# Latent attention of a hybrid encoder: prompt tiles taken from the last (512 keys) to the first (128 keys)

## What is computed

```python
q_n = m_qn.reshape(b, t, MLA_HEADS, MLA_NOPE_DIM)          # 64 wide
q_p = rope(m_qr.reshape(b, t, MLA_HEADS, MLA_ROPE_DIM), pos)  # 32 wide
k_n = jnp.einsum('bsc,chd->bshd', c_all, mla_w_uk)
v_c = jnp.einsum('bsc,chd->bshd', c_all, mla_w_uv)
s = (jnp.einsum('bqhd,bkhd->bhqk', q_n, k_n)
     + jnp.einsum('bqhr,bkr->bhqk', q_p, k_pe)).astype(jnp.float32) * MLA_SCALE
s = jnp.where(mask, s, -jnp.inf)      # prompt: key_chunk <= q_chunk, chunks of 64
probs = jax.nn.softmax(s, axis=-1).astype(v.dtype)
o = jnp.einsum('bhqk,bkhd->bqhd', probs, v)
```

## Time and profile before

| what | value |
|---|---|
| runs | 1555.78, 1557.09, 1557.13 us; median 1557.09 us |
| profiled execution, its own time | 1557.62 us |
| its span (first to last instruction) | 1555.8 us |
| PE, DVE, POOL, ACT busy | 97%, 66%, 53%, 44% of the span |
| MLA stage in layer 0 | iteration 18 begins at 236.24 us, the last output part at 308.00 us |
| PE's idle time in that stage | 0.99, 0.76, 0.84 and 0.59 us |
| granted clock of PE | 1.00 in that stage, 0.997 over the span |

### The profile page before, as it was taken

One profiled execution on the slowest core, in us unless ns is written; L12 is line 12 of the kernel. 1 busy time (PEld: TensorE's weight loads), 2 busy tenths in 40 slices (PEclk: granted clock), 3 DMA queues, 4 the chain that ended last, 5 costly groups with the idle time before them and its releaser, 6 DMA issues.

```text
span 1555.8 us, 33898 instructions
## 1 busy us (share of the span) xinstructions
PE 1512.2 (97%) x14202; PEld 1432.6 (92%) x14202; DVE 1027.9 (66%) x1750; ACT 681.4 (44%) x1204; POOL 832.3 (53%) x468
## 2 busy tenths in 40 slices
PE   7999999999999999999999999999999999999997
PEld 6989888799999999999998898878999999999996
DVE  6866556646848668586677655675488594766955
ACT  6621434344534344455455223344454443434553
POOL 3344111175765949578643441113659477594973
PEclk9999999999999999999999999999999999999998
DMA  6211011243241422322322110114323324142122
GB/s 204 70 54 41 17 58 42 51 118 96 77 140 42 137 68 86 105 68 98 103 80 69 43 43 15 58 46 70 113 92 95 96 75 140 46 136 68 46 91 85
DMA packets 45128, 123.81 MB, mean 80 GB/s; under 512 B 10992, under 2 KB 15856, under 8 KB 44720
## 3 DMA queue, kind: packets, MB, share of 16 engines
q1 hardware_dynamic: 44688, 119.86, 25.7%
q10 hardware_dynamic: 288, 1.78, 0.3%
HBM read 117.86 MB, written 3.76 MB: 78 GB/s over the span
## 4 chain that ended last, share of the span: by engine, by line
PE 77%; DVE 13%; POOL 5%; ACT 3%; issue 2%; DMA 0%; SPq 0%; DVEq 0%; ACTq 0%; POOLq 0%
PE psum_p L1811 38%; PE psum_t L1868 17%; PE psum_p L1884 6%; PE psum_t L1920 6%; POOL w_rest L810 3%; DVE conv_out L1339 2%; PE psum_p L1847 2%; PE psum_p L2068 1%; PE psum_p L2048 1%; POOL w_rest L798 1%; PE psum_t L2032 1%; PE psum_t L2039 1%; PE psum_t L1904 1%; DVE mla_q L1369 1%; PE psum_p L1904 1%
## 5 line engine op out<-in xcount | busy, mean ns | idle before, releaser
L1811 PE MATMUL psum_p<-hidden,w_high 128*128 128x272 f32 x3680 | 618.3, 290 | 5.4 <-POOL w_rest L798 4.1
L1811 PEld LDWEIGHTS psum_p<-hidden,w_high 128*128 128x128 f32 x3680 | 519.5, 188 | 10.3 <-POOL w_rest L798 6.0
L798 POOL TENSOR_TENSOR w_rest<-raw,w_high 128x1024 fp32r<-128x1024 f32 x110 | 268.9, 2448 | 397.6 <-ACT w_high L927 397.6
L1811 PE MATMUL psum_p<-hidden,w_rest 128*128 128x272 f32 x1840 | 379.8, 288 | 0.0
L1811 PEld LDWEIGHTS psum_p<-hidden,w_rest 128*128 128x128 f32 x1840 | 288.4, 188 | 0.0
L810 POOL TENSOR_TENSOR w_rest<-w_sums,w_high 128x512 fp32r<-128x512 f32 x128 | 208.0, 1650 | 93.3 <-DVE w_sums L1594 55.3
L927 ACT ACTIVATE w_high<-raw 128x1024 fp32r<-128x1024 f32 x112 | 117.9, 1055 | 153.7 <-PE psum_p L1811 103.4
L1868 PE MATMUL psum_t<-hidden_split_a,w_high 128*128 128x272 f32 x896 | 178.6, 290 | 2.1 <-issue 1.0
L1868 PE MATMUL psum_t<-hidden_split_b,w_high 128*128 128x272 f32 x896 | 177.0, 288 | 0.4 <-DVE hidden_split_b L1610 0.4
L1868 PEld LDWEIGHTS psum_t<-hidden_split_a,w_high 128*128 128x128 f32 x896 | 140.0, 188 | 5.8 <-issue 4.5
L1868 PEld LDWEIGHTS psum_t<-hidden_split_b,w_high 128*128 128x128 f32 x896 | 140.3, 188 | 0.8 <-DVE hidden_split_b L1610 0.8
(11 more groups left out here) (307 smaller groups left out, 2627.2 us busy)
## 6 DMA issues: line engine op xcount, KB each, us to landing
raw<-w_units SPq DMA_DIRECT2D x146, 512.0 KB, 3.6
raw_more<-w_units SPq DMA_DIRECT2D x64, 512.0 KB, 3.5
x<-x_t SPq DMA_DIRECT2D x8, 272.0 KB, 6.7
y_t<-y SPq DMA_DIRECT2D x8, 272.0 KB, 2.2
constants<-consts ACTq DMA_DIRECT2D x1, 1088.0 KB, 9.3
ple_in<-p_t SPq DMA_DIRECT2D x2, 544.0 KB, 11.7
constants<-consts SPq DMA_DIRECT2D x1, 1088.0 KB, 6.1
constants<-consts ACTq DMA_DIRECT2D x1, 649.5 KB, 6.2
```

Source lines behind the costliest of these rows:

```text
L798: mark(pool.tensor_tensor(wlo_at(l, s, 2), raw_at(l, u), whi_at(l, s, 2).bitcast(F32), ALU.subtract), lo_done)
L1811: ins = pe.matmul(pp[:, 2 * b + h, 0:HALF], w(l, s, 2)[:, cols(k)], rhs[:, k, part, h * HALF:(h + 1) * HALF], start=(n == 0 and z == 0), s ...
```

## The change

The prompt's MLA tasks come in the order of tiles 3, 2, 1, 0, and the sample's four stay last. Tasks 18 to 21 then have 512 keys, 22 to 25 have 384, 26 to 29 have 256 and 30 to 33 have 128. All else in the schedule stays at its iteration. The second hunk keeps the PSUM bank's wait on the tile that was split before. No instruction is added or removed.

```diff
+MLA_ORDER = (3, 2, 1, 0, 4)
+
+
 def tasks():
     out = [("swa", n, g) for n in range(NCH) for g in range(2)]
-    out += [("mla", i, h) for i in range(SEQ // P + 1) for h in range(4)]
+    out += [("mla", i, h) for i in MLA_ORDER for h in range(4)]
     return out
...
                 rows, first_key, keys = task_shape(kind, i)
-                last_group = [mixed.at(l, i if kind == "swa" else NCH + i)] if h1 == 1 and t > 1 else []
+                last_group = [mixed.at(l, i if kind == "swa" else NCH + MLA_ORDER.index(i))] if h1 == 1 and t > 1 else []
                 wait_apart(pe, pcopy.at(l, t + 1), *last_group)
```

## The result

The changed kernel takes 1564.29 us (median of five runs, 1562.66 to 1564.42), against 1557.13 us before (five runs, 1555.78 to 1557.68). The ratio is 1.0046, with a 95% interval of 1.0036 to 1.0057: 7.2 us slower. The forecast was 1562.8, in a range from 1556.8 to 1566.8.

A forecast was written before the change was run, and what follows sets the result against it. PE, 97% busy, was taken as the bound, except in B, set by DVE. A +5.6, B -1.8, C -1.0 make +2.8 us a layer, +5.7 in two, giving 1562.8 us; range 1556.8 to 1566.8.

The forecast's parts named there:

- B: Latent attention, 271.58 to 294.71 us, until output feature tile 1 starts: set by DVE, 23.13 falls to 21.34 us.
- The long wait: PE's wait for DVE before the output part's tile 1, forecast as most of 4.4 us of waits in B.
- POOL's hold: In B, DVE scalings started inside POOL's rest end only after it: 1.50 us against 0.49.
- Both scalings that were to be held: DVE's scalings of tasks 28 and 32 in B, forecast to end after POOL's rests; the 128-key one 1.3 to 1.5 us.
- A: Latent attention, 233.42 to 271.58 us, to the last quarter of iteration 28's unit: PE-bound, longer by 5.6 us a layer.
- the scores' price: PE's scores per task: 512 keys 0.56 us above 128, 384 keys 0.11 above 256; +2.35 us in A.
- C: Latent attention, 294.71 to 308.00 us, until the last tiles start: PE's own, shorter by 1.0 us a layer.
- the turn of task 33 and the values: PE's work in C: turn of task 33 and values of 32 and 33, -0.33 - 0.65 = -1.0 us.
- No change: Rival, chance 0.18: PE, busiest over the whole span, keeps all its work; time 1557 to 1559 us.
- Faster: Rival, chance 0.12: DVE reaches `mixed_a` before PE, both PE waits in B vanish, -1.60 us a layer; 1553.9 us.
- Much slower: Rival, chance 0.05: 512-key tasks meet chain steps; PE waits about 1 us in each of iterations 18 to 25; 1573 us.

The follow-up runs named there:

- dve_B: Changed kernel plus two unused DVE operations of 128x544 in iteration 31 of each layer, inside B; 1568.78 us.
- late_after: Changed kernel, but ACT rounds the second output unit's weights in iteration 35, not 32, so POOL's rest moves out of B; 1562.90 us.
- last0: Kernel before, with the prompt's tiles in the order 1, 2, 3, 0; 1561.62 us, ratio 1.0036.
- last3: Kernel before, with the prompt's tiles in the order 2, 1, 0, 3; 1561.45 us, ratio 1.0034.
- the filled kernel: Changed kernel plus five unused fp32 PE matmuls of 128x256 a layer, where PE waits in B; 1562.77 us, ratio 1.0040 to the kernel before.

## Why the prediction was right, and which terms were off

The order costs 2.84 us a layer by the forecast and 3.47 by the rows at full clock. The difference, 1.3 us in two layers, is most of what lies between the forecast 1562.8 and the measured 1564.29.

**B, the main step, held.** PE's work in it was forecast at 16.9 us and measured 16.93; its waits at 4.4 and 4.26; B at 21.34 and 21.20. The long wait ended with L1312, and the waits for ACT lay before scores and a turn. But the long wait was 1.70 us of the 4.26, not most of it. The waits for ACT came to 2.01, and a wait of 0.55, at the values of the next tile, was not foreseen: they write the PSUM bank that DVE was still splitting. That DVE sets B is shown by dve_B, that POOL's hold lies in its chain by late_after. Both scalings that were to be held were held. The second took 1.70 us and not 1.3 to 1.5. Of a rest of 2.38 us 1.49 would have been left at 0.89 us after its start, and the scaling of rows 12 ended 0.29 behind its rest, so the rows themselves gave 1.8. The rest took 2.51, of which 1.62 lay after the scaling's start, and 0.08 came behind it.

**A was mis-sized, +6.0 for +5.6.** The failed term is the scores' price. The earlier trace rows gave 604 and 326 ns, but these stood in two places: 512 keys in B, 128 keys in A. After the change each size stands in the other's place:

```profile
L2042 PE MATMUL psum_t<-mla_k,mla_q 96*128 96x512 f32 x8 | 4.5, 644 | 0.0
L2042 PE MATMUL psum_t<-mla_k,mla_q 96*128 96x384 f32 x8 | 3.6, 538 | 0.0
...
L2042 PE MATMUL psum_t<-mla_k,mla_q 96*128 96x256 f32 x8 | 2.4, 379 | 0.0
L2042 PE MATMUL psum_t<-mla_k,mla_q 96*128 96x128 f32 x8 | 1.6, 286 | 1.1 <-ACT probs L1061 1.1
```

At one place 512 keys cost 644 - 326 = 318 ns a record more than 128, thus 0.64 us a task and not 0.56; 384 and 256 differ by 0.21 (538 and 431, 485 and 379) and not 0.11. With these A's scores come to 4 x 0.64 + 4 x 0.21 - 3 x 0.21 = +2.8 in place of 2.35, and that is the missing 0.4. Turns and values were right. The same error sat in B's PE work: the scores' busy time there fell by 2.75 us (6.34 to 3.59) and not by 2.35. Yet PE's as a whole fell by 4.60, as forecast, so something of some 0.4 us, not traced, made up for it, and the 16.9 was met in part by luck. It would not have moved B's end, which is DVE's.

**C was mis-sized, -0.6 for -1.0.** The term is "the turn of task 33 and the values". PE's work in C fell by 0.89 us (12.70 to 11.81) and not by 0.98, and PE's idle time there grew by 0.30 (0.59 to 0.89): 0.20 us of it before the second output unit, for ACT's last exponential, is the part that the waits show. Where the other 0.1 us lies was not traced.

**The clock was not in the prediction at all.** It cost 1.5 us in layer 0 of the profiled run (C 14.19 against 12.70), and in none of the three later profiles with the same gaps. So 2 x 3.5 = 7.0 us of stage growth is what the order costs, and the 7.2 measured between the medians agrees with it. The upper end of the range, 1566.8, had been set for another reason, waits in A that did not come; a fall that costs 1.5 us in both layers would have carried the time past it (1557.1 + 7.0 + 3.0 = 1567.1).

**The rivals.** No change, by PE's share over the whole span, fell with B, where PE's work shrank by 4.6 us and the stretch by 1.9. Faster fell since DVE sheds less than PE per task, and PE's waits in B grew from 1.60 to 4.26 us where this rival had them vanish. (Its PE share of "about 1.5 us" for a 512-key task over a 128-key one is 1.2 by the prediction's own prices: 0.56, 0.33 and 0.32.) Much slower, by waits beside the chain, fell: A's gaps stayed at 0.99 us (44.18 - 43.19).

## What to carry to other kernels

When work is moved between stretches, price it on every engine, and ask in each stretch which engine sets its end: what leaves a stretch that another engine bounds is not gained there, but is paid in full where the moved engine is the bound. A second engine's share of 66% over the span says little, if it is 94% in the one stretch that counts. And take the price of an operation at the place where it will stand; two sizes measured in two places differ by their places too.

## What was not expected of the hardware

PE's clock fell from 2.4 to 1.2 GHz (granted clock 0.50 of full) for a short stretch once PE had waited in B: in eight layers of eight with 4.3 us of waits there, in both of dve_B, in both of late_after (19.77 - 16.93, thus some 2.8 us of waits at full clock), in one of two in last0 (2.5 us), in none of two in last3 (3.2 us), in one of six with the gaps filled (2.1 us left) and in none of six with the order of before. So the sum of the waits alone does not decide it. Its sign in the timeline is a group of four matmuls of 272 columns that takes 1.25 us, four rows after one of the same kind that took 0.77; the window view of the changed kernel has the clock:

```profile
297.31 0.77 PE L1907 MATMUL psum_p<-hidden,w_high 128*128 128x272 f32 x4 [1.70 <-DVE hidden L1312]
...
299.01 1.25 PE L1907 MATMUL psum_p<-hidden,w_high 128*128 128x272 f32 x4
```

```profile
299.00:301.00 2.00, 2.00 (x10) 2.00 (x11) 0.86 (x3) 0.74 (x3) 0.00 (x0) 0.50 0.00 0
```

Where the fall lands changes from one execution to the next, and so does its price, from 0 to 1.5 us. The Trainium skill (TensorE: Matmul & The Clock Gate, Part 1: The HAM clock gate) says that a low clock is the default, that activity lifts it, and that the place of the change varies between runs. The traces agree: PE's first groups of four take 1.11 us and later ones 0.67, and the level rose near 18.6 us in one profile and near 15.6 in the other. That rise is worth as much as a fall: between profiles it moved the beginning of the stage by 1.2 to 2.2 us. For a change of a few us this is a spread that filling the gaps makes rarer in B (one layer of six against eight of eight) but, going by the filled kernel's runs, does not remove.
